# A router stretch rebuilt, and a weight part loaded later, ahead of a weight stream

## The reference

```python
# second layer, end of the mixer
y_d = (rms_norm(o) * silu(z)) @ w_delta
h = h + (sigmoid(gate_f) * y_f + sigmoid(gate_d) * y_d) @ w_out
# mixture of experts: 64 experts in 8 groups, width 256, two experts for each token
hn = rms_norm(h, norm2_g)
gl, el = hn @ w_rg + b_rg, hn @ w_re + b_re       # group logits, expert logits
group = top_1(softmax(gl)); experts = top_2(softmax(el of that group))
for each expert e: out[its tokens] += weight * (silu(x @ w_gate[e]) * (x @ w_up[e])) @ w_down[e]
```

## Time and profile before

| | us |
|---|---|
| median of 3 runs | 1172.59 |
| lowest and highest of them | 1170.87, 1176.24 |
| the profiled execution, its own time | 1179.27 |
| span of that execution in the trace | 1176.0 |
| PE busy | 1028.1 (87%) |
| DVE, ACT, POOL busy | 505.4, 381.2, 427.2 |
| DMA engines, mean rate over the span | 259 GB/s |

### The profile page before, as it was taken

One profiled execution on the slowest core, in us unless ns is written; L12 is line 12 of the kernel. 1 busy time (PEld: TensorE's weight loads), 2 busy tenths in 40 slices (PEclk: granted clock), 3 DMA queues, 4 the chain that ended last, 5 costly groups with the idle time before them and its releaser, 6 DMA issues.

```text
span 1176.0 us, 20192 instructions
## 1 busy us (share of the span) xinstructions
PE 1028.1 (87%) x8177; PEld 808.9 (69%) x8177; DVE 505.4 (43%) x979; ACT 381.2 (32%) x571; POOL 427.2 (36%) x192
## 2 busy tenths in 40 slices
PE   8999999999999999999999989976766766767686
PEld 6999999999999999797989788342322322323232
DVE  4347966601146886766854633121111111111113
ACT  5554354444457656334243434110000000000002
POOL 6767778888876775142031371000000000000000
PEclk9999999999999999999999999998888888888888
DMA  7644546566655544115220977999999999999995
GB/s 249 218 136 146 172 135 181 179 185 191 181 177 179 180 144 142 38 37 215 85 77 22 362 303 294 356 426 428 428 428 428 428 428 428 428 428 428 428 423 224
DMA packets 43570, 304.75 MB, mean 259 GB/s; under 512 B 5093, under 2 KB 5477, under 8 KB 30441
## 3 DMA queue, kind: packets, MB, share of 16 engines
q1 hardware_dynamic: 43208, 303.21, 68.3%
q10 hardware_dynamic: 288, 0.52, 0.1%
HBM read 302.67 MB, written 1.05 MB: 258 GB/s over the span
## 4 chain that ended last, share of the span: by engine, by line
PE 57%; DMA 26%; DVE 9%; issue 2%; POOL 2%; SPq 2%; ACT 2%; DVEq 0%; ACTq 0%; POOLq 0%
DMA arena<-gate_up 24%; PE bank L481 11%; PE bank L483 11%; PE bank L482 11%; PE bank L1351 7%; PE bank L859 5%; PE bank L1372 3%; DMA weights<-front 1%; PE bank L823 1%; DVE arena L2078 1%; POOL rounded L2903 1%; DMA arena<-down 1%; SPq L2988 1%; PE bank L1094 1%; PE bank L1073 1%
## 5 line engine op out<-in xcount | busy, mean ns | idle before, releaser
L2903 POOL TENSOR_TENSOR rounded<-weights,rounded 128x1024 fp32r<-128x1024 f32 x152 | 370.1, 2462 | 159.8 <-ACT rounded L1437 150.5
L481 PE MATMUL bank<-rounded 128*128 128x256 f32 (+2 forms) x776 | 219.4, 283 | 2.8 <-POOL rounded L2903 2.0
L482 PE MATMUL bank<-rounded 128*128 128x256 f32 (+2 forms) x776 | 216.5, 279 | 0.0
L483 PE MATMUL bank<-rounded 128*128 128x256 f32 (+2 forms) x776 | 216.4, 279 | 0.0
L1437 ACT ACTIVATE rounded<-weights 128x1024 fp32r<-128x1024 f32 x146 | 147.2, 1052 | 83.1 <-PE bank L483 52.0
L481 PE MATMUL bank<-rounded,rounded 128*128 128x256 f32 (+3 forms) x552 | 159.9, 290 | 2.3 <-DVEq L2333 0.7
L483 PE MATMUL bank<-rounded,rounded 128*128 128x256 f32 (+3 forms) x552 | 157.5, 285 | 0.0
L482 PE MATMUL bank<-rounded,rounded 128*128 128x256 f32 (+3 forms) x552 | 157.4, 285 | 0.0
L481 PEld LDWEIGHTS bank<-rounded 128*128 128x128 f32 (+1 forms) x776 | 145.4, 187 | 5.2 <-POOL rounded L2903 2.7
L483 PEld LDWEIGHTS bank<-rounded 128*128 128x128 f32 (+1 forms) x776 | 145.5, 188 | 0.0
L482 PEld LDWEIGHTS bank<-rounded 128*128 128x128 f32 (+1 forms) x776 | 145.2, 187 | 0.3 <-issue 0.2
(11 more groups left out here) (462 smaller groups left out, 1458.4 us busy)
## 6 DMA issues: line engine op xcount, KB each, us to landing
weights<-front SPq DMA_DIRECT2D x165, 512.0 KB, 4.3
arena<-down SPq DMA_DIRECT2D x31, 2048.0 KB, 21.8
weights<-gate_up SPq DMA_DIRECT2D x28, 2048.0 KB, 34.1
arena<-gate_up SPq DMA_DIRECT2D x28, 2048.0 KB, 33.6
weights<-front SPq DMA_DIRECT2D x4, 2048.0 KB, 8.0
arena<-gate_up SPq DMA_DIRECT2D x4, 1536.0 KB, 34.3
weights<-gate_up SPq DMA_DIRECT2D x4, 1024.0 KB, 14.2
weights<-gate_up SPq DMA_DIRECT2D x4, 768.0 KB, 8.2
```

Of the source, the lines that this page charges most:

```text
L481: nc.tensor.matmul(out, a[0], b[1], start=start, stop=False)
L482: nc.tensor.matmul(out, a[0], b[0], start=False, stop=False)
L483: return nc.tensor.matmul(out, a[1], b[0], start=False, stop=stop)
L2903: nc.gpsimd.tensor_tensor(lo, raw[q % RAW], hi.bitcast(f32), ALU.subtract).then_inc(sem("w_lo"), 1)
```

## The change

What it does:
- Parts 2, 7 and 12 get their place in the region of `k_tok` instead of `v_tok`. Part 2 is loaded after the wait for `gd_part(7)`, together with parts 3 and 4, no longer ahead of `w_router` and the first expert weights. ACT's order is not changed: `round_part(2)` still stands ahead of `norm_sqrt("no")`.
- Parts 5 to 9 are loaded in one go; the two loads of `gate_up` for group 1 that stood ahead of parts 8 and 10 now stand ahead of parts 10 and 11. A third one (`[1]`) goes out right behind the first load after `merged2`, and the fourth (`[0]`) waits for the sums of squares.
- The products of parts 14 and 15 go to two banks. The residual sum, the squares, the logits and the sums of their two chunks are done one by one.
- The filling products are gone. The transposes of `res` stand in their place, the first between the last two logit steps and three among the transposes of `m_T`.
- The first half of the gathered block is signalled on its own (`xg_hi`); products for k = 0 to 3 start with it, and those from k = 4 on wait for the second half (`lows`). ACT runs a one-column `Silu` ahead of the loop.
- Group 2's loads are cut at k = 1, 3, 5 instead of 1, 4.

The core of the diff:

```diff
-        part_at = [RING + v_tok_at if i == 4 else 2 * i * QUARTER for i in range(5)]
+        home_at = k_tok_at
+        part_at = [RING + home_at if i == 4 else 2 * i * QUARTER for i in range(5)]
...
-                last.then_inc(full[f.b] if n % 2 else sem("parts"), 1)
+                last.then_inc(full[f.b] if n % 2 or n == 14 else sem("parts"), 1)
...
             wp_part(7)
-            keep_busy("busy0", 2)
-            router_part(3)
-            sums_part(3)
-            pe.wait_ge(sem("h2"), 8)
+            router_part(3, (6,))
+            sums_part(3, (6,))
+            token_quarter(0, (4,))
+            router_part(3, (7,))
+            sums_part(3, (7,))
+            pe.wait_ge(sem("h2"), 9)
             for t in range(TT):
                 for i in range(2):
+                    if t == i == 1:
+                        for n, x in ((1, sums_of[0]), (2, logits_of[0]), (3, logits_of[1])):
+                            token_quarter(n, (x.b,))
...
-            keep_busy("busy1", 2)
             pe.wait_ge(sem("r_steps"), 1)
...
-            for i in range(4):
-                f = begin(f"x{i}", (4 + i,))
-                for j in range(4):
-                    last = nc.tensor.transpose(...)
-                end(f, last)
-            for b in range(4):
+            for b in PJ:
                 pe.wait_ge(free[b], uses[b])
...
-                pe.wait_ge(sem("xg"), 2 * m + 2)
+                if 0 in ks:
+                    pe.wait_ge(sem("xg_hi"), m + 1)
...
                 for k in ks:
+                    if k == KD // 2:
+                        pe.wait_ge(sem("lows"), 2 * m + low)
...
-                    if u == 0 and k in (0, KD // 2 - 1):
+                    if u == 0 and k in (0, 2, 4):
                         last.then_inc(sem("part_used"), 1)
...
                 it = p * N_GROUPS
+                nc.scalar.activation(unread[0][:, 0:1], ones[:, 0:1], ACT.Silu)
                 gathered_hi(it)
...
             sp.wait_ge(sem("o_b"), 4)
-            load_part(2)
             sp.dma_start(w_router, A["w_router"]).then_inc(sem("router_in"), 16)
             load_gate_up(0, 0, [0])
             load_down_first(0, 0)
             last = readers[f"block{GD + 1}"]
             sp.wait_ge(full[last.b], last.n + 1)
+            load_part(2)
             load_part(3)
             load_part(4)
             load_down_second(0)
-            for n in (5, 6, 7): load_part(n)
+            for n in range(5, 10): load_part(n)
             load_gate_up(1, 1, [2])
-            for n in (8, 9): load_part(n)
+            load_part(10)
             load_gate_up(1, 1, [3])
-            for n in range(10, N_PARTS): load_part(n)
+            for n in range(11, N_PARTS): load_part(n)
             sp.wait_ge(sem("merged2"), 4)
             load_gate_up(0, 0, [1])
+            load_gate_up(1, 1, [1])
             part_done(14)
             load_gate_up(0, 0, [3])
             part_done(15)
             load_gate_up(0, 0, [2])
-            load_gate_up(1, 1, [0, 1])
-            last = fills["router1"]
-            sp.wait_ge(full[last.b], last.n + 1)
+            for name in ("router1", "ssq41"):
+                sp.wait_ge(full[fills[name].b], fills[name].n + 1)
+            load_gate_up(1, 1, [0])
...
             sp.wait_ge(sem("part_used"), 2)
-            load_even_part(2, 1, KD // 2)
+            load_even_part(2, 1, 3)
+            sp.wait_ge(sem("part_used"), 3)
+            load_even_part(2, 3, 5)
             sp.wait_ge(sem("gate_up"), 3)
-            load_even_part(2, KD // 2, KD)
+            load_even_part(2, 5, KD)
```

More of the change, by code:

```diff
@@ L383, in build @@
         y_sum_hi_r = h1_lo_r
-        part_at = [RING + v_tok_at if i == 4 else 2 * i * QUARTER for i in range(5)]
-        set_raw = [arena[:, v_tok_at:v_tok_at + QUARTER] if i == 4 else weights[:, 2 * i * QUARTER:(2 * i + 1) * QUARTER]
+        home_at = k_tok_at
+        part_at = [RING + home_at if i == 4 else 2 * i * QUARTER for i in range(5)]
+        set_raw = [arena[:, home_at:home_at + QUARTER] if i == 4 else weights[:, 2 * i * QUARTER:(2 * i + 1) * QUARTER]
                     for i in range(5)]
@@ L396, in part_in @@
             return sem(PART_IN[part_set(n)]), PART_BEFORE[part_set(n)] + 16 * (n // 5 + 1)
-        assert r_values_end + KD * SEQ <= top[0] - 1
-        h_sq = arena[:, r_values_end:r_values_end + KD * SEQ].rearrange("p (k t) -> p k t", k=KD)
+        h_pairs = [arena[:, at:at + 2 * SEQ].rearrange("p (k t) -> p k t", k=2)
+                   for at in (v_tok_at, v_tok_at + 2 * SEQ, v_tok_at + 4 * SEQ, r_values_end)]
+        assert r_values_end + 2 * SEQ <= home_at and v_tok_at + 6 * SEQ <= ARENA - 6 * BLOCK
         xg = m_T.rearrange("p k t -> p (k t)")[:, 0:D].rearrange("p (k s) -> p k s", k=KD)
@@ L1228, in wp_part @@
             def wp_part(n):
-                f = begin(f"wp{n // 2}", PJ) if n % 2 == 0 else fills[f"wp{n // 2}"]
+                f = begin(f"wp{n // 2 + n // 7}", PJ) if n % 2 == 0 or n == 7 else fills[f"wp{n // 2}"]
                 part_product(f, 8 + n, (y_sum_hi_r, y_sum_lo_r))
@@ L1237, in _, with router_part, sums_part, token_quarter @@
             sums_of = [begin(f"ssq4{t}") for t in range(TT)]
-            def router_part(j):
-                pe.wait_ge(sem("h2"), 2 * j + 1)
+            def router_part(j, ks=None):
+                pe.wait_ge(sem("h2"), 2 * j + 1 if ks is None else ks[0] + 1)
                 for t, f in enumerate(logits_of):
-                    for k in (2 * j, 2 * j + 1):
+                    for k in ks or (2 * j, 2 * j + 1):
                         last = nc.tensor.matmul(f.bank[:, 0:72], res[:, k, META + t * P:META + (t + 1) * P], w_router[:, k, :],
                                                 start=k == 0, stop=k == KD - 1)
-                    if j == 3:
+                    if k == KD - 1:
                         end(f, last)
-            def sums_part(j):
-                pe.wait_ge(sem("squares"), 13 + j + 1)
+            def sums_part(j, ks=None):
+                pe.wait_ge(sem("squares"), 13 + j + 1 if ks is None else 11 + ks[0])
                 for t, f in enumerate(sums_of):
-                    for k in (2 * j, 2 * j + 1):
-                        last = nc.tensor.matmul(f.bank[:, 0:1], h_sq[:, k, t * P:(t + 1) * P], ones[:, 0:1],
+                    for k in ks or (2 * j, 2 * j + 1):
+                        last = nc.tensor.matmul(f.bank[:, 0:1], h_pairs[k // 2][:, k % 2, t * P:(t + 1) * P], ones[:, 0:1],
                                                 start=k == 0, stop=k == KD - 1)
-                    if j == 3:
+                    if k == KD - 1:
                         end(f, last)
[L1259 to L1263, removed]
+            def token_quarter(i, pool):
+                f = begin(f"x{i}", pool)
+                for j in range(4):
+                    last = nc.tensor.transpose(f.bank[:, j * P:(j + 1) * P],
+                                               res[:, 4 * (i // 2) + j, META + i % 2 * P:META + (i % 2 + 1) * P], ident)
                 end(f, last)
-                pe.sem_inc(free[f.b], 1)
-            omasks = tri[:, 0:4 * P]
             router_part(0)
@@ L1399, in _ @@
                 gather(it, 4 * it + 2)
-                for b in range(4, 8):
+                for b in WK:
                     pe.wait_ge(free[b], uses[b])
-                first_products(it, 0)
+                first_products(it, 0, low=1)
                 with pe.Fori(0, N_GROUPS // 2 - 1) as pair:
@@ L1419, in _ @@
                 scatter(it + 1, (0,))
[L1420 removed]
+                scatter(it + 1, (1,), 2)
                 read_count(pe, count)
@@ L1847, in _, with token_quarter @@
             round_part(13)
-            for j in range(4):
+            def token_quarter(i):
+                f = fills[f"x{i}"]
+                link(nc.scalar.activation(of_quarter(i), f.bank[:, :], ACT.Copy))
+                act.sem_inc(free[f.b], 1)
+            for j in range(3):
                 act.wait_ge(sem("h2"), 2 * j + 1)
-                nc.scalar.activation(h_sq[:, 2 * j:2 * j + 2, :], res[:, 2 * j:2 * j + 2, META:], ACT.Square).then_inc(sem("squares"), 1)
+                nc.scalar.activation(h_pairs[j], res[:, 2 * j:2 * j + 2, META:], ACT.Square).then_inc(sem("squares"), 1)
                 if j == 0:
@@ L1856, in _ @@
             nc.scalar.activation(spare[:, 0:1], ones[:, 0:1], ACT.Sqrt)
+            for k in (6, 7):
+                act.wait_ge(sem("h2"), k + 1)
+                nc.scalar.activation(h_pairs[3][:, k - 6, :], res[:, k, META:], ACT.Square).then_inc(sem("squares"), 1)
             act.wait_ge(sem("variance"), 6)
@@ L1875, in _ @@
             for i in range(4): got(f"x{i}")
-            for i in range(4):
-                link(nc.scalar.activation(of_quarter(i), fills[f"x{i}"].bank[:, :], ACT.Copy))
-                act.sem_inc(free[fills[f"x{i}"].b], 1)
+            for i in range(4): token_quarter(i)
             def gathered_hi(m):
```

(16 more changed lines are left out.)

25 lines of the change are left out of this document (12 added, 13 removed).

## The result

| | before | after |
|---|---|---|
| median of 5 runs, us | 1173.69 | 1183.78 |
| lowest to highest | 1170.87 to 1176.24 | 1181.04 to 1184.53 |
| profiled execution, own time | 1179.27 | 1181.04 |
| its span | 1176.0 | 1179.3 |

The ratio of the times is 1.0082 (95% interval 1.006 to 1.0105): the change makes the kernel about 9.6 us slower (7.0 to 12.3). I had forecast +1.7 us and a highest time of 1181.0; the result lies beyond it.

A forecast was written before the change was run, and what follows sets the result against it. PE's chain was taken to bound the kernel up to about 760 us, the weight stream after it. Terms 6.5 - 2.7 - 1.7 - 0.4 = +1.7 us on 1172.59 gave 1174.3 us, range 1168 to 1181.

The forecast's parts named there:

- The late part: Part 2, rounded on ACT ahead of the square root, lands later and delays the root: +10.5 us (9.7 to 11.7).
- The cold restart: PE restarts at the low clock after 10.7 us idle, mostly hidden by ACT's and DVE's steps: +0.5 us.
- Parts 8 and 9, and part 11: PE's wait for parts 8 and 9 and its low clock go, -5.0 us; part 11 comes late, +0.5 (0 to 2).
- rival 3: The 2 MB loads ahead of parts 10 and 11 hold PE 3 to 4 us: +3 on the sum, 1177.3; 12%.
- The router stretch and the first groups: First product -2.7 us; smaller gap and full clock in first group's products -1.7; half signal before second group -0.4.
- rival 2: PE's clock stays low through `wd0` and falls again in the router stretch, gather and first products: +7.9 us, 1180.5; 18%.
- the refill: SP's loads released by PE's second products of the first group; the end moves by what they move: +1.7 us.
- the weight loads' row: PE's waits for parts 8, 9 and 11 around the moved 2 MB loads: -5.0 and +0.5 us.

The follow-up runs named there:

- the second trace: The changed kernel, unchanged, profiled once more: 1184.67 us in a single execution.
- after_gu3_later: Changed kernel, with the second `gate_up` load for group 1 issued behind part 12 instead of ahead of part 11: 1180.92 us, ratio 1.0061 to the kernel before.
- after_both_filler: Changed kernel, part 2 rounded behind the four roundings, second `gate_up` load behind part 12, two filling products between ranks and gather: 1169.69 us, ratio 0.9967.
- before_part2_late: Kernel before, with only part 2's load moved behind the wait for `gd_part(7)`: 1186.30 us, ratio 1.0113.
- after_round2_moved: Changed kernel, with ACT rounding part 2 behind the four roundings instead of ahead of the square root: 1171.65 us, ratio 0.997 to the kernel before.
- after_both: Changed kernel, with part 2 rounded behind the four roundings and the second `gate_up` load behind part 12: 1168.43 us, ratio 0.996 to the kernel before.
- after_oldloads: Changed kernel, with group 1's two `gate_up` loads back ahead of parts 8 and 10: 1180.71 us, ratio 1.0072 to the kernel before.
- after_round2_oldloads: Changed kernel, part 2 rounded behind the four roundings, group 1's two `gate_up` loads back ahead of parts 8 and 10: 1169.75 us, ratio 0.9973.

## Why the prediction was wrong

**The late part.** Foreseen as the main cost, and it is. I put the landing between 4.3 and 6.3 us after the issue and took 5.1; it was 6.10 us in the first trace after, and 5.44 to 5.98 in the four others with the late load ahead of the root. Taking the 512 KB of part 2 out of what lies ahead brought 0.2 to 0.9 us, not the 1.2 of its bytes. The root came 11.5 us late (10.9 in the second trace) instead of 10.5, within my bounds.

**The cold restart.** Priced 0.5. The first issue behind `wd0` was 11.8 us late, 0.3 more than the root. Right.

**Parts 8 and 9, and part 11: the step that failed.** I wrote -5.0 for a wait and a low clock that go, and +0.5 for part 11, together -4.5. Measured they are -3.5 and +4.3, together +0.8; with the 0.3 of the cold restart that is the +1.1 of B against the first trace (+1.6 against the mean of three, 49.83). Two terms were mis-sized. First, the -5.0 supposed that part 9's rest would be ready just in time, with landings of 4.3 us. Part 5 took 5.54 to land, and behind it POOL needs 2.4 us for each of five parts, one after the other; I had counted POOL's last step, not its queue. The wait shrank by 2.4 us to 0.85, another of 0.64 for part 5 came up (0.28 before), and the low clock went: SP's issue behind the products of parts 8 and 9 (700.02 after, 696.00 before) is 8.3 us late where `wd0` was 11.8 late, so -3.5. Second, part 11 cost 2.58 us of waiting and a low clock behind it, 12.6 - 8.3 = 4.3 us by the first router product, against 0.5 with a bound of 2. I had its landing time after 9 us; it took 11.42, with two 2 MB loads and part 10 ahead of it. And I did not apply to it my own finding, that a wait near 3 us also costs the clock. This was rival 3, with its mechanism as stated and a price of +3 on my sum where +3.8 was measured; it got 12%. The trace of `after_gu3_later` shows that taking the load away takes the wait away.

**The router stretch and the first groups.** Forecast -2.7, -1.7 and -0.4, together -4.8; C shows -4.6 in the first trace, and -2.4, -1.7 and -0.5 one by one (31.29 us from the first router product to the first group's before, 28.84 after). The sum is right. The way is not quite: the gather did fall to the low clock, as rival 2 said, and lost 1.6 us, but most of that was in the shade of ACT's chain, as `after_both_filler` shows (0.4 us at the refill).

**The sum.** +11.5 + 1.1 - 4.6 = +8.0 by the two traces, against +1.7. Of the 6.3 us of the miss 1.0 is the landing, 5.3 the weight loads' row, and the rest small terms that nearly cancel. The timed runs put the change another 1.6 us higher; the spread of B in the kernel before covers that, no more is shown.

**The range.** Its upper end was built from rival 2 alone, and the 2 us by which medians vary were given to the low end only. The weight loads' row at its measured size (about +5 on my sum), the later landing (+1) and those 2 us reach 1182.3, still 1.5 below the median.

**Confirmed.** The end is set by the refill (D within 2 us in twelve traces). The place of a single 512 KB load in SP's order moves the root by 11.4 us where ACT wants it ahead of the root (`before_part2_late`). In the first trace after, the granted clock is 0.50 from 658 on, PE takes up work at 664.78, and the clock is 0.66 between 670 and 672 and 1.00 after. The rule of the Trainium skill (TensorE: Matmul & The Clock Gate, Part 1) that activity releases the throttled clock fits this restart.

**Left open.** Whether moving the two loads costs 1.6 us or nothing: one pair of traces says the first, the other the second, and the timed runs can't tell. Whether part 2 rounded between the root and the four roundings would spare the wait for part 5 was not tried. The early loads of `gate_up` `[1]` and the cut of group 2's loads were not tried by themselves.

## What to carry to other kernels

Where a load is put behind a wait, look for the first instruction of an in-order engine that needs it, and for what stands behind that instruction: here a square root that had nothing to do with the weights. One moved line on ACT turned a loss of 0.8% into a gain of 0.3%. The moved work then has a new neighbour: follow it through the engines behind it too, here POOL and DVE, where it cost 2.2 us that I had not looked for. A large prefetch put ahead of a small urgent load moves the wait to the next small load, and a part that goes through two more engines must be costed by the queue of the slower of them, not by its last step.

## What was not expected of the hardware

- A load of 512 KB issued 9 us behind 4 MB of others landed 5.4 to 6.1 us after its issue; the first of two such loads issued together into an empty queue took 4.7 us in the kernel before, 4.82 in `after_gu3_later` and 5.54 in the first trace after.
- The clock fell although PE was not idle for long. In `after_round2_moved` it worked between two gaps of 0.99 and 1.76 us, and the gather behind them ran at 0.50 from 727 to 733. In `after_both`, two filling products in the second gap brought the gather back from 5.36 to 3.83 us. Nor did the length of a gap decide: behind a wait of 2.43 us (`after_round2_moved`) and one of 2.38 (`after_oldloads`) the clock fell to 0.50, behind 2.41 (`after_round2_oldloads`) and 2.19 (`after_both`) it stayed at 1.00.
- With the queue otherwise empty, the first cut of group 2's loads, whose rows are short (256 KB on 128 partitions, 2 KB each), moved at most 330 GB/s, with the DMA engines counted as busy for most of the time, where whole blocks run at 428. That the short rows are the cause was not tested (stretches of 1 us in `after_round2_moved`):

```profile
736.00:737.00 1.00, 1.00 (x16) 0.28 (x11) 0.00 (x0) 0.00 (x0) 0.00 (x0) 1.00 0.81 238
737.00:738.00 1.00, 1.00 (x16) 0.37 (x12) 0.00 (x0) 0.00 (x0) 0.00 (x0) 1.00 0.95 330
738.00:739.00 1.00, 1.00 (x15) 0.26 (x8) 0.00 (x0) 0.00 (x0) 0.00 (x0) 1.00 1.09 330
```
